# Two attention stages of one inference step on one core: prompt latent attention in V-stationary form with scaling first, and a reordered end of layer 1

## What is computed

```python
def mla_attend(q_lat, q_pe, kv, q_pos):
    c_kv, k_pe = kv[..., :MLA_KV_LORA], kv[..., MLA_KV_LORA:]
    s = jnp.einsum('bqhc,btc->bhqt', q_lat, c_kv) + jnp.einsum('bqhr,btr->bhqt', q_pe, k_pe)
    s = s.astype(F32) * (MLA_NOPE + MLA_ROPE) ** -0.5
    k_pos = jnp.arange(kv.shape[1])
    s = jnp.where(k_pos[None, :] <= q_pos[:, None], s, -jnp.inf)
    p = jax.nn.softmax(s, axis=-1).astype(kv.dtype)
    return jnp.einsum('bhqt,btc->bqhc', p, c_kv)
...
    wts = jax.nn.softmax(jnp.stack(lses), axis=0)
    o = jnp.einsum('gblh,gblhe->blhe', wts, jnp.stack(outs).astype(F32)).astype(x.dtype)
    return o.reshape(b_sz, l_len, MIX_C) @ w_out, rows
```

## Time and profile before

| | us |
|---|---|
| median of 3 runs | 3666.47 (3664.84 to 3669.62) |
| profiled execution | 3665.12, span 3663.2 |
| prompt latent attention | 446.8 to 679.1 |
| decode pages begin | 684.9 |
| layer 1, dense stretch with half 4's units | 2499.8 to 2619.8 |
| layer 1, last half (`pe_last`, its loop) | 2619.8 to 2711.6 |
| rest of the output projection | 2711.6 to 2801.8 |
| second FFN | from 2801.8 |

### The profile page before, as it was taken

The page is one execution under the profiler, slowest core; times in us unless marked ns, Lnnn a source line. Parts: engine busy times, 40 slices in busy tenths (PEclk is TensorE's granted clock), DMA queues, the critical chain, the costliest instruction groups (busy, mean ns, idle before and its releaser), DMA issues. The chain is left out here.

```text
span 3663.2 us, 44774 instructions
## 1 busy us (share of the span) xinstructions
PE 3403.8 (93%) x18200; PEld 2498.2 (68%) x18200; DVE 1722.7 (47%) x3701; ACT 630.1 (17%) x1628; POOL 62.8 (2%) x90
## 2 busy tenths in 40 slices
PE   9999889767989999999989999999877999999997
PEld 5675556545558777776877867767653777777676
DVE  0216455687254333457751223224565433335777
ACT  1214233233120000000120111112223000000002
POOL 0000000011000000000000000000000000000000
PEclk9999799899999999999999999999987999999998
DMA  3120100397321111011221111212210111111122
GB/s 133 35 58 1 62 17 1 141 352 300 124 69 47 46 46 46 34 60 64 95 81 41 63 53 51 91 37 83 92 35 23 46 46 42 39 46 60 64 85 103
DMA packets 63528, 266.55 MB, mean 73 GB/s; under 512 B 6288, under 2 KB 24728, under 8 KB 52352
## 3 DMA queue, kind: packets, MB, share of 16 engines
q1 hardware_dynamic: 55072, 176.94, 14.0%
q0 software_dynamic: 8288, 87.30, 6.3%
HBM read 246.29 MB, written 17.93 MB: 72 GB/s over the span
## 5 line engine op out<-in xcount | busy, mean ns | idle before, releaser
L512 PE MATMUL ps<-arena 128*128 128x344 f32 (+1 forms) x4928 | 1081.2, 383 | 13.8 <-ACT arena L553 12.0
L512 PEld LDWEIGHTS ps<-arena 128*128 128x128 f32 x4928 | 831.7, 191 | 264.5 <-issue 23.2
L759 PE MATMUL ps<-arena 128*128 128x344 f32 (+1 forms) x2464 | 539.5, 381 | 1.5 <-DVE arena L678 1.5
L759 PEld LDWEIGHTS ps<-arena 128*128 128x128 f32 x2464 | 414.6, 190 | 127.2 <-DVE arena L678 3.4
L1937 PE MATMUL ps<-arena 128*128 128x344 f32 x1152 | 352.8, 463 | 15.5 <-ACT arena L352 5.7
L1937 PEld LDWEIGHTS ps<-arena 128*128 128x128 f32 x1152 | 219.7, 194 | 134.5 <-issue 24.5
L216 PE MATMUL ps<-arena 128*128 128x344 f32 x672 | 198.7, 459 | 8.7 <-DMA arena<-in_w_a 8.7
L1948 PE MATMUL ps<-arena 128*128 128x256 f32 (+1 forms) x864 | 206.3, 395 | 0.0
L1948 PEld LDWEIGHTS ps<-arena 128*128 128x128 f32 (+1 forms) x864 | 178.8, 263 | 23.4 <-issue 6.0
L555 ACT ACTIVATE arena<-arena 128x688 f32<-128x688 f32 (+1 forms) x88 | 55.7, 633 | 756.4 <-DVE arena L617 756.4
L216 PEld LDWEIGHTS ps<-arena 128*128 128x128 f32 x672 | 129.5, 193 | 77.2 <-DMA arena<-in_w_a 8.7
(11 more groups left out here) (321 smaller groups left out, 3670.5 us busy)
## 6 DMA issues: line engine op xcount, KB each, us to landing
arena<-in_w_fi SPq DMA_DIRECT2D x44, 1024.0 KB, 4.8
arena<-in_w_fo SPq DMA_DIRECT2D x16, 1536.0 KB, 6.3
arena<-in_w_fo SPq DMA_DIRECT2D x16, 1280.0 KB, 5.6
arena<-in_w_out_a SPq DMA_DIRECT2D x24, 512.0 KB, 3.5
arena<-in_w_qk SPq DMA_DIRECT2D x24, 512.0 KB, 3.5
arena<-in_c SPq DMA_DIRECT2D x6, 2048.0 KB, 11.7
arena<-in_x SPq DMA_DIRECT2D x6, 1376.0 KB, 10.1
arena<-in_w_a SPq DMA_DIRECT2D x14, 512.0 KB, 3.5
```

The lines of the kernel that those rows point to most:

```text
L512: mm = pe.matmul(ps[:, BANK[p], 0:HALF[s]], prod[j][p][0], prod[j][p][1], start=(j == 0), stop=(j == 3))
L759: mm = pe.matmul(ps[:, BANK[p], 0:HALF[s]], prod[p][0], prod[p][1], start=(j == 0), stop=(j == NKP - 1))
```

## The change

In the FFN's start, the first two products of the first unit go ahead of `pe_ln_sum`. In latent attention the units of two heads alternate; the probabilities are scaled by the inverse sum on ScalarE ahead of the transposes (`norm`), V becomes the stationary operand and the transposed probabilities stream, the two heads' results go to the two halves of the partitions, and the result needs no further transposes. `KH` and `SP_` become four-fold, `PT` double. TensorE's order is now turn(u), scores(u+2), values of a pair; VectorE's inverse(u+1), mask(u+2), finish(u). In layer 1 the mask's additions and maximum become one instruction per head; Pool weights and adds the stored groups; half of the last decode queries and products become four more dense steps of half 5; the output projection starts one iteration later and takes in the decode values and two layer norms in a new order over banks 0, 1, 4 and 6.

```diff
@@ -517,19 +517,26 @@
             out_tiles = 3 + 3 * (tb_before // 2) + 12
             pe.wait_ge(free[0], out_tiles)
             pe.wait_ge(free[1], out_tiles)
-            pe_ln_sum(pe, n_ln, 2)
             for q, (n, s) in enumerate(IN_UNITS[:4]):
                 pe.wait_ge(loaded[n], 16 * ((LB_FI0, LB_FI1)[l] // 2 + 1))
-                pe.wait_ge(st_w, W_IN[l] + 4 * (n + 1))
-                pe.wait_ge(st_t, T_IN[l] + 4 * (s + 1))
+                if q:
+                    pe.wait_ge(st_w, W_IN[l] + 4 * (n + 1))
+                    pe.wait_ge(st_t, T_IN[l] + 4 * (s + 1))
 
                 def need(p):
+                    if q == 0 and p == "p1":
+                        normed(n_ln)(pe, 0)
+                    if q == 0 and p == "p6":
+                        pe.wait_ge(st_w, W_IN[l] + 4)
+                        pe.wait_ge(st_t, T_IN[l] + 4)
                     if q and p == "p1":
                         pe.wait_ge(st_g, G_IN[l] + 2 * (q - 1) + 1)
                     elif q:
                         pe.wait_ge(st_e, E_IN[l] + 7 * (q - 1) + IN_FREES[p])
 
                 def between(p):
+                    if q == 0 and p == "p2":
+                        pe_ln_sum(pe, n_ln, 2)
                     if q == 0 and p == "p7":
                         pe_ln_var(pe, n_ln, 2)
...
         def pe_mla_values(pe, units):
             for tt in units:
...
+        KEYS_AT = {5: 0, 11: 1}
...
-                    pe.wait_ge(m_tc, NT * (h - 1))
+                    pe.wait_ge(m_tc, MU.index((h - 2 - h % 2, QORDER[0])) + (6, 12)[h % 2])
...
-                pe.wait_ge(m_p, u + 1)
-                if u % NT == 0:
-                    pe.wait_ge(kh_cp, h + 2 if h + 1 < NH else h + 1)
+                pe.wait_ge(m_n, u + 1)
+                pe.wait_ge(kh_cp, made[0])
                 if u:
                     pe.wait_ge(m_tc, u)
...
-            def values(u):
+            def values(w):
+                h, i = MU[2 * w]
+                pe.wait_ge(m_tc, 2 * w + 2)
+                if w == 0:
+                    pe.wait_ge(v_cp, NT)
+                if w >= 2:
+                    pe.wait_ge(m_oc, w - 1)
+                for j in range(i + 1):
+                    for q in range(2):
+                        mm = pe.matmul(ps[64 * q:64 * q + 64, 6 + w % 2, 0:P], V[:, j, (h + q) * 64:(h + q) * 64 + 64],
+                                       PT[q][:, j * P:(j + 1) * P], start=(j == 0), stop=(j == i))
+                mm.then_inc(m_o, 1)
+
+            keys(0)
+            pe.wait_ge(kh_cp, 1)
+            keys(1)
+            scores(0)
+            scores(1)
+            for u, (h, i) in enumerate(MU):
+                turn(u)
+                if u + 2 < len(MU):
+                    scores(u + 2)
+                if u % 2:
+                    values(u // 2)
+                if u % 16 in KEYS_AT and h + 2 < NH:
+                    keys(h - h % 2 + 2 + KEYS_AT[u % 16])
+            pe.wait_ge(m_oc, len(MU) // 2)
+            leave("pe", pe)
+
...
-            keys(0)
-            for u, (h, i) in enumerate(MU):
-                if u == 0:
-                    scores(0)
-                    pe.wait_ge(kh_cp, 1)
-                    keys(1)
+                act.wait_ge(m_ng, u + 1)
+                act.activation(SP_[u % 4][:, 0:(i + 1) * P], SP_[u % 4][:, 0:(i + 1) * P], ACT.Exp,
+                               bias=m_neg[:, u % 4:u % 4 + 1], scale=MLA_SCALE,
+                               accum_out=m_sum[:, u % 4:u % 4 + 1]).then_inc(m_p, 1)
+
+            def norm(u):
+                h, i = MU[u]
+                act.wait_ge(m_iv, u + 1)
+                act.mul(SP_[u % 4][:, 0:(i + 1) * P], SP_[u % 4][:, 0:(i + 1) * P], m_inv[:, u % 4:u % 4 + 1]).then_inc(m_n, 1)
+
+            def output(w):
+                h, i = MU[2 * w]
+                act.wait_ge(m_o, w + 1)
+                act.copy(MO[:, h // 2, i * P:(i + 1) * P], ps[:, 6 + w % 2, 0:P]).then_inc(m_oc, 1)
+
+            soft(0)
+            soft(1)
+            norm(0)
+            for u in range(len(MU)):
                 if u + 1 < len(MU):
-                    scores(u + 1)
-                turn(u)
-                if u:
-                    values(u - 1)
-                if u % NT == NT - 1 and h + 2 < NH:
-                    keys(h + 2)
-            values(len(MU) - 1)
...
-            output(len(MU) - 2)
-            output(len(MU) - 1)
-            act.wait_ge(m_oc, len(MU))
+                    norm(u + 1)
+                if u + 2 < len(MU):
+                    soft(u + 2)
+                if u % 2 and u > 1:
+                    output(u // 2 - 1)
+            output(len(MU) // 2 - 1)
+            act.wait_ge(m_oc, len(MU) // 2)
...
                 dve.wait_ge(m_s, u + 1)
-                if u >= 2:
-                    dve.wait_ge(m_t, u - 1)
-                    dve.wait_ge(m_p, u - 1)
+                if u >= 4:
+                    dve.wait_ge(m_t, u - 3)
+                    dve.wait_ge(m_n, u - 3)
...
+
+            def inverse(u):
...
             def finish(u):
                 h, i = MU[u]
                 nk = (i + 1) * P
-                dve.wait_ge(m_p, u + 1)
+                dve.wait_ge(m_t, u + 1)
                 if u >= 2:
-                    dve.wait_ge(m_oc, u - 1)
-                dve.reciprocal(m_inv[:, u % 2:u % 2 + 1], m_sum[:, u % 2:u % 2 + 1]).then_inc(m_iv, 1)
-                dve.wait_ge(m_t, u + 1)
-                if u >= 1:
-                    dve.wait_ge(m_o, u)
+                    dve.wait_ge(m_o, u // 2)
                 pv = ps[:, 4:6, :].rearrange("p a b -> p (a b)")[:, 0:nk]
-                dve.tensor_copy(PT[:, 0:nk], pv).then_inc(m_tc, 1)
+                dve.tensor_copy(PT[u % 2][:, 0:nk], pv).then_inc(m_tc, 1)
...
+            inverse(0)
             for u, (h, i) in enumerate(MU):
                 if u + 1 < len(MU):
-                    mask(u + 1)
+                    inverse(u + 1)
+                if u + 2 < len(MU):
+                    mask(u + 2)
                 finish(u)
-                if u % NT == NT - 1 and h + 2 < NH:
...
-                if i == 5:
+                if i == 4:
                     sp_cached_keys(sp, 2)
...
+            elif d - D_KEYS >= len(key_units(i)):
+                pair = d - D_KEYS - len(key_units(i))
+                pe_query(pe, 2, 2 * pair, b)
+                pe_query(pe, 2, 2 * pair + 1, b).then_inc(t_ps, 1)
...
-                pe.wait_ge(a_add, 2 * n)
+                pe.wait_ge(a_add, 4 * n)
...
-            for a in range(2):
-                dve.tensor_tensor(DS[n % 2][:, a::2, 0:nk],
-                                  ps[:, a, :].rearrange("p (b k) -> p b k", k=2 * P)[:, :, 0:nk],
-                                  BIAS[i % 2][:, a::2, 2 * P - nk:2 * P], ALU.add).then_inc(a_add, 1)
-            dve.wait_ge(a_add, 2 * (n + 1))
...
-            link("dve", dve, dve.tensor_reduce(mx, DS[n % 2][:, :, 0:nk], AX.X, ALU.max))
+            for j in range(4):
+                off = (j // 2) * 2 * P
+                dve.tensor_tensor_reduce(DS[n % 2][:, j, 0:nk], ps[:, j % 2, off:off + nk], BIAS[i % 2][:, j, 2 * P - nk:2 * P],
+                                         1.0, NEG, ALU.add, ALU.max, mx[:, j:j + 1]).then_inc(a_add, 1)
+            dve.wait_ge(a_add, 4 * (n + 1))
...
-            dve.wait_ge(c_w, v + 1)
-            for q in (1, 2):
-                o4 = r[:, q, 0:256].rearrange("p (h e) -> p h e", h=4)
-                ins = dve.tensor_tensor(o4, o4, ce[:, q, :, None].to_broadcast([P, 4, HD]), ALU.mult)
-            link("dve", dve, ins)
-            link("dve", dve, dve.tensor_tensor(r[:, 1, 0:256], r[:, 1, 0:256], r[:, 2, 0:256], ALU.add))
...
+            dve.wait_ge(others, OTHERS0 + 3 * v + 3)
...
+            def stored_sum(v):
+                r, ce = OR[v % 4], CE[v % 2]
+                pool.wait_ge(c_w, v + 1)
+                pool.wait_ge(c_in[v % 3], 16 * (v // 3 + 1))
+                for q in (1, 2):
+                    o4 = r[:, q, 0:256].rearrange("p (h e) -> p h e", h=4)
+                    pool.tensor_tensor(o4, o4, ce[:, q, :, None].to_broadcast([P, 4, HD]), ALU.mult).then_inc(others, 1)
+                pool.wait_ge(others, OTHERS0 + 3 * v + 2)
+                pool.tensor_tensor(r[:, 1, 0:256], r[:, 1, 0:256], r[:, 2, 0:256], ALU.add).then_inc(others, 1)
...
-        OC_BANK = [6] * 8 + [6, 4] * 4 + [4, 5, 6, 2] * 2
+        OC_BANK = [6] * 5 + [0, 1, 6] + [0, 1, 6, 4] * 2 + [0, 6, 1, 4] * 2
...
-        FIRST_CHUNK = {6: (0,), 7: (1,), 8: (2,), 9: (3,), 10: (4, 5), 11: (6, 7)}
+        OUT_C_AT = {7: ((0, 0), (0, 1)), 8: ((0, 2), (0, 3), (0, 4)), 9: ((0, 5), (0, 6), (0, 7)),
+                    10: ((1, 0), (1, 1)), 11: ((1, 2), (1, 3))}
+        REST_OF_C1 = range(4, 8)
 
         def pe_last(pe):
             for it in range(NU + 4):
                 if it < NU:
                     pe_scores(pe, 5, it)
-                if it < 4:
-                    pe_query(pe, 2, 2 * it, 6)
```

(62 more changed lines are left out.)

196 lines of the change are left out of this document (100 added, 96 removed).

## The result

The changed kernel takes 3778.24 us (median of 4, 3774.83 to 3782.26) where the kernel before takes 3668.05 beside it: ratio 1.030, 95% interval 1.0282 to 1.0318. The forecast was 3705, in a range of 3645 to 3770; the direction was right, the size was not. The profiled execution has a span of 3773.0 us for 3663.2, so 109.8 us have to be found.

The account below looks back on a forecast made before the run. Two places decide: latent attention, where TensorE is full, and layer 1's end, where it isn't. 3663.2 + 76 (latent) - 5 (FFN start) - 32 (end) = 3702 span, 3705 median; range 3645 to 3770.

Parts of the forecast that it names:

- The ring: Latent attention: transposes, scores, mask, copy and next transposes wait for each other without overlap; 3.48 us a pass, 64 passes 223 us.
- T: Latent attention: a unit's transposes on TensorE, priced at 0.47 us a pass.
- F: Latent attention: VectorE's copy out of the transposed block, 0.90 us a pass with 0.14 of handover to TensorE.
- The ring's sum: Latent stage at full clock: 223 us of passes, 31 of values, 30 and 10 of key projections, 294 us together.
- a possible 9 us: Latent attention: TensorE's drain at tiling-mode changes, a 0.27 us tail for each of 32 returns, left to the upper bound.
- The clock: Latent stage: granted clock 0.9, costing 20 us, with bounds of 8 us (0.96) and 50 us (0.78).
- half clock through most of the ring: Rival, latent attention: large units run at 1.2 GHz for most of their TensorE work, +130 instead of +76; chance 0.17.
- Values: Latent attention: value products in two array halves overlap in full, 0.053 us each, 31 us in all.
- FFN starts: Start of each layer's FFN: the next unit starts 5 us sooner, -5 for layer 0, layer 1's in its end.
- The wait of 6.02 us: FFN start: the next unit's wait was to shrink from 6.02 us to one or two.
- End of layer 1: Dense stretch to second FFN unit: dense +3.4, loop 98 us for 91.8, FFN unit 80 after it; -32 together, -15 to -60.
- Pool: Layer 1's last-half loop: group sums fit in Pool's free time, up to 1.7 us for each of three operations.

Follow-up runs that it names:

- e7: Changed kernel with 1 to 11 products of 128 unread columns behind scores(u+2), 1.3 us in the mean: 3709.8 us, ratio 1.0112 to the kernel before.
- e3: Changed kernel with 1 to 8 products of 128 unread columns behind scores(u+2), 0.96 us in the mean: 3701.66 us, ratio 1.0102 to the kernel before.
- e12: Changed kernel with 1 to 4 products of 128 unread columns behind scores(u+2), 0.5 us in the mean: 3701.92 us, ratio 1.0099 to the kernel before.

## Why the prediction was right and wrong

**The ring was right.** T follows F by 0.15 us all through the timeline, and with the clock restored a pass lasts what the terms say. Of e7, four and five blocks:

```profile
529.12 0.63 PE L1325 MATMUL ps<-arena 128*128 128x128 f32 x4 [1.36 <-issue]
529.59 1.25 PE L1314 MATMUL ps<-arena 96*128 96x512 f32 x4
530.67 1.50 PE L1355 MATMUL ps<-arena 128*128 128x128 f32 x12
530.87 0.82 DVE L1418 CUSTOM_DVE_ANT_0 arena<-ps,arena 128x640 f32<-128x640 f32 x1 [1.78 <-PE ps L1314]
...
531.82 0.69 DVE L1435 COPY arena<-ps 128x512 f32<-128x512 f32 x1
...
532.65 0.63 PE L1325 MATMUL ps<-arena 128*128 128x128 f32 x4 [0.48 <-DVE arena L1435]
...
536.09 1.09 PE L1338 MATMUL ps<-arena 128*64 128x128 f32 x16 [0.39 <-DVE arena L1435]
...
537.12 0.76 PE L1325 MATMUL ps<-arena 128*128 128x128 f32 x5
```

3.53 us from T to T. By the terms: 0.42 + (1.07 + 0.27) + (0.82 + 0.12) + (0.69 + 0.14) = 3.53.

**The ring's sum was about 5 us short.** At a clock of 0.95 the stage is 309 us (e3, e7, e12), where the sum had 294. Not all of the 15 us is the ring: two pieces are half clock that the filling didn't reach. The first key projection, ahead of the loop, ran at half clock (6.39 us, the second 3.65) and lost some 3 us; in the changed kernel:

```profile
446.85 6.39 PE L1299 MATMUL ps<-arena 128*64 128x512 f32 x8 [2.65 <-DVEq L2764]
...
454.55 3.65 PE L1299 MATMUL ps<-arena 128*64 128x512 f32 x8 [1.31 <-DVE arena L1403]
...
461.39 0.33 PE L1325 MATMUL ps<-arena 128*128 128x128 f32 x1 [1.40 <-ACT arena L1372]
```

And the first four passes got no products (`if u >= 4`). Two stretches of e7 show it; the columns are those of the earlier trace rows:

```profile
463.00:486.90 23.90, 16.57 (x67) 10.22 (x66) 7.11 (x20) 7.14 (x13) 0.00 (x0) 0.50 0.00 1
486.90:750.00 263.10, 230.29 (x1718) 174.65 (x1716) 108.04 (x296) 100.46 (x203) 0.00 (x0) 1.00 0.00 1
```

The first five passes of e7 last 28.2 us, the same five of the next two heads, at full clock, 20.5: another 7.7 us. So some 10 of the 15 us are the clock, and 5 are left to the sum. More than that is named by two items: the first turn began 14.6 us into the stage and not 10, 2 us more than the slow key projection explains, and the return from the values costs 6. At 0.053 us a record, the 16 records that begin at 536.09 in e7 end at 536.94, and the next transposes begin at 537.12, 0.18 later, 32 times. I had named that as a possible 9 us and left it to the upper bound. The Trainium skill, page "TensorEngine Tiling (Array Packing)", section Key Properties, has each change of tiling mode drain TensorE. The trace agrees: in e7 transposes begin 0.20 us after the last value record, and the key projections, whose tiles have 64 columns like the values', 0.10 us after it; so the change itself is 0.10 us of the 0.18, and the rest is spacing that 0.053 a record leaves out. The scores that follow transposes, without such a change, come with next to no gap (644.50 above: 0.69 after a start of six blocks of 0.105). Together the two items are 3 us more than there are to explain; other terms were too high by as much, and no run separates them.

**The clock was the step that failed.** "Between them I take 0.9" put the stage between the decode pages (0.94) and the end of layer 1 (0.78) and priced the loss at 20 us, at most 50. It was granted 0.66 and lost 388 - 309 = 79 us that the filling gave back, and some 10 more that it didn't reach. Three things were wrong in it. The first is a reading of the order: "For eight blocks the new ring leaves TensorE a gap of 0.27 + 1.35 + 1.36 = 3.0 us in every pass" adds the mask and the copy of two large units, but the order puts the mask of a small unit beside the copy of a large one and the other way round (three and seven blocks above). So no gap of 3.0 us occurs; the longest in the stage is 2.3 us, and most are 1.7 to 2.0, whatever the unit. That "such falls should recur with the large units" rested on it; in fact the passes of small and large units have about the same gap. The second is the comparison by how long TensorE idles altogether. In the kernel before, the decode pages have gaps of 1.61 us with 5 us of nearly unbroken work between two of them, and the end's loop has gaps of 3 to 6 us with 4 to 13 us of work between; in the ring, at full clock, 1.6 us (595.37 to 596.97 above) to 4 us of work lie between two gaps. That this is what matters is my reading of the rows; no run varied it alone. The third is that half clock feeds itself here: TensorE's half of the ring doubles where VectorE's doesn't shrink, so more of the time is spent at it. Of my rivals "half clock through most of the ring" was the right one, and it too confined the fall to the large units: +130 for 149.8. The Trainium skill, page "TensorE: Matmul & The Clock Gate", section on oscillation, cited there, was the better guide than the two rows I went by, though the waits of its worked case are longer than any gap of this ring; the rival deserved more than 0.17. The row, with its gap of 2.24 us and scores at half clock behind it, was the one row of the same kind of loop; to price the stage by it, scores, turns and values all doubled in each pass, would have given some 150 us more than 294, too much, but the range would have reached over the result.

**Values: right.** 28 records of 128 columns took 1.75 us less a tail of 0.27, 0.053 each: two tiles ran together in full, as the quarters had the earlier trace rows. The 31 us stand. At half clock they take twice that.

**FFN starts: right in layer 0, too high in layer 1.** In layer 0 5.7 us, by the variance matmul. The wait of 6.02 us ahead of the next unit, which I said would shrink to one or two, is 6.02 still: it lasts from the end of the two products behind the variance matmul until that chain is through, and both moved together. In layer 1 I left out that the products need their weights: the row above shows them at 2.75 us behind a transfer. In the changed kernel they are late too, and the sum matmul waits for VectorE anyway:

```profile
2906.44 6.56 PE L512 MATMUL ps<-arena 128*128 128x344 f32 x16 [3.73 <-issue]
...
2916.71 1.41 PE L304 MATMUL ps<-arena 128*128 128x344 f32 x2 [3.72 <-DVE arena L314]
```

**End of layer 1: right, each piece.** Dense stretch +4.1 (forecast 3.4), loop 100.2 (98), from the loop to the second FFN unit 81.7 (80); the variance matmuls came 17.0, 38.3 and 70.3 us after the loop (17, 37, 68). Together -26.8 for -32. Inside the loop two errors cancelled: a mask's four instructions are spaced 0.35 us and not 0.45, so VectorE was sooner, and the output steps and decode values filled TensorE more closely than "VectorE-bound, then TensorE-bound" had it. What I didn't see is that the same masks help the four halves before, by 5 us.

**Pool: right.** The first two rows of Pool in the last half:

```profile
2781.64 1.18 POOL L2227 TENSOR_TENSOR arena<-arena 128x256 f32<-128x256 f32 x2 [27.28 <-DVE arena L2175]
2782.89 0.72 POOL L2229 TENSOR_TENSOR arena<-arena 128x256 f32<-128x256 f32 x1
```

Elsewhere the pair takes 1.32, so 2.04 us a unit and some 0.7 an operation, well under the 1.7 us for each of three operations (over 5 us a unit) that I called free. VectorE's waits in the loop name Pool nowhere, as they should. Against VectorE's 0.76 + 0.42 that is a factor of 1.7; the page "GPSIMD Engine Reference" of the Trainium skill, section 3.1, gives 1.96 for a longer add, by which I had 2.5.

**The total.** The parts outside the stage came to -40 by the trace for -37. The stage alone was 74 us longer than its 314. 69 of them are the clock, which cost 89 us (79 given back by the filling, some 10 left in it) where I had 20; about 5 are the ring's sum. The parts outside take 3 off again, and what remains to the 73 of the medians is below what a measurement tells.

## What to carry to other kernels

When a change closes a ring between two engines, price it twice: once at full clock, as the sum of its steps, and once with TensorE's steps at half clock, and let the range reach from the one to the other; a gap in every pass cost some 80 to 90 of 388 us here; 0.2 us of useless products in it brought 64 back, 0.5 us 79. Before moving a product forward in a queue, ask for all of its inputs, weights too: the early FFN products waited for theirs. And if two engines alternate, look at both queues for the step that could be issued one place earlier or later: scores one place forward and values one place back, no instruction added or removed, made this stage 178 us shorter.

## What was unexpected about the hardware

A single product of 0.2 us a pass raised the stage's granted clock from 0.66 to 0.90, and with standing times of 1.5 to 1.7 us in each pass it was at 2.4 GHz nearly throughout, where with 1.7 to 2.0 us it was at 1.2 GHz two thirds of the time. It is no fixed boundary: in the changed kernel, too, some gaps of 1.8 to 2.0 us had full clock right behind them. The stage's mean clock was 0.66 though TensorE was busy in 261.7 of its 387.9 us. In e7 a change from 64-column tiles to full ones cost 0.10 us. On VectorE, instructions that follow one another overlap a little: in the mask, 128x256 elements with the running maximum took 0.42 us but followed one another every 0.35 us.
